# Output projection as split fp32r products, latents' low parts on GpSimd, later expert loads

## What is computed

```
z = rms_norm(x) @ w_in                      # (512, 1440): q_a, k_a, v_a, c_q, c_kv, k_rope
o_a = window_gqa(q_a, k_a, v_a, ...)        # 8 heads, 4 blocks of 128 queries, a band of keys
q   = rms_norm(c_q)  @ w_qb                 # (512, 384) @ (384, 768)
kv  = rms_norm(c_kv) @ w_kvb                # (512, 256) @ (256, 1024)
o_b = latent_attention(q, kv, k_rope)       # 8 heads, all 512 keys
o   = concat(rms_norm(o_a), rms_norm(o_b))
x   = x + o @ w_o                           # (512, 1024) @ (1024, 1024)
h2  = rms_norm(x);  x = x + expert_choice_ffn(h2, ...)   # 16 experts, 64 tokens each
mod = silu(c) @ w_mod + b_mod               # (1, 1024) @ (1024, 6144), used by the second block
```

## Time and profile before

| what | value |
|---|---|
| time, three runs | 1559.26, 1560.69, 1561.72 us; median 1560.69 |
| the profiled execution's own time | 1559.61 us |
| its span | 1557.8 us (the page's times lie inside this span) |
| busy: PE, weight load, DVE, ACT, POOL | 94%, 61%, 40%, 32%, 4% of the span |
| DMA | 310.27 MB, mean 199 GB/s |

### The profile page before, as it was taken

One profiled execution on the slowest core, in us unless ns is written; L12 is line 12 of the kernel. 1 busy time (PEld: TensorE's weight loads), 2 busy tenths in 40 slices (PEclk: granted clock), 3 DMA queues, 4 the chain that ended last, 5 costly groups with the idle time before them and its releaser, 6 DMA issues.

```text
span 1557.8 us, 17583 instructions
## 1 busy us (share of the span) xinstructions
PE 1459.2 (94%) x7133; PEld 956.3 (61%) x7133; DVE 616.2 (40%) x1188; ACT 490.8 (32%) x904; POOL 69.4 (4%) x96
## 2 busy tenths in 40 slices
PE   8988988998999999999996999988898999999998
PEld 6855466454433433333323899966686888888886
DVE  5366666334122222122115542125675443254325
ACT  6355376331001101100103412357734333123321
POOL 2000000000000000000001200000001101000100
PEclk9989999999999999999998999989999999999999
DMA  7477350427999999999995122140021332233211
GB/s 231 81 306 280 131 208 1 149 104 283 423 420 422 421 421 421 421 421 422 421 421 201 41 89 75 55 162 1 10 86 54 109 108 76 87 108 108 101 35 54
DMA packets 82738, 310.27 MB, mean 199 GB/s; under 512 B 7188, under 2 KB 43309, under 8 KB 55906
## 3 DMA queue, kind: packets, MB, share of 16 engines
q1 hardware_dynamic: 80656, 305.34, 50.2%
q10 hardware_dynamic: 1202, 2.15, 1.2%
q0 software_dynamic: 800, 1.66, 0.3%
HBM read 303.35 MB, written 5.78 MB: 198 GB/s over the span
## 4 chain that ended last, share of the span: by engine, by line
PE 73%; DMA 14%; DVE 6%; ACT 5%; issue 1%; SPq 0%; DVEq 0%; ACTq 0%
PE ps L433 13%; PE ps L434 13%; PE ps L435 13%; PE ps L805 13%; DMA sb<-in_w_gate 5%; DMA sb<-in_w_up 5%; PE ps L663 4%; DMA sb<-in_w_down 2%; PE ps L932 1%; PE ps L757 1%; DMA raw<-in_a_w_in 1%; ACT sb L1068 1%; PE ps L530 1%; PE ps L574 1%; PE ps L620 1%
## 5 line engine op out<-in xcount | busy, mean ns | idle before, releaser
L805 PE MATMUL ps<-sb 128*64 128x512 f32 x1536 | 352.5, 599 | 15.7 <-DMA sb<-in_w_gate 5.4
L805 PEld LDWEIGHTS ps<-sb 128*64 128x64 f32 x1536 | 102.9, 136 | 222.2 <-issue 178.6
L1068 ACT ACTIVATE sb<-ps 128x512 f32<-128x512 f32 (+4 forms) x176 | 90.7, 530 | 342.5 <-PE ps L757 88.3
L434 PE MATMUL ps<-r_fl,r_top 128*128 128x512 f32 x344 | 135.1, 393 | 0.0
L435 PE MATMUL ps<-r_act,r_low 128*128 128x512 f32 x344 | 134.8, 392 | 0.0
L433 PE MATMUL ps<-r_act,r_top 128*128 128x512 f32 x344 | 134.3, 390 | 0.0
L2096 DVE TENSOR_TENSOR r_low<-raw,r_top 128x2048 fp32r<-128x2048 f32 x33 | 74.2, 2289 | 78.7 <-ACT r_top L1068 78.7
L1874 DVE TENSOR_TENSOR sb<-sb,ps 128x512 f32<-128x512 f32 x64 | 43.7, 687 | 139.6 <-PE ps L794 139.6
L433 PE MATMUL ps<-r_low,r_h 128*128 128x256 f32 x288 | 82.5, 287 | 1.0 <-ACT sb L1068 1.0
L1068 ACT ACTIVATE r_top<-raw 128x2048 fp32r<-128x2048 f32 x33 | 61.4, 1907 | 69.7 <-PE ps L435 69.7
L434 PE MATMUL ps<-r_low,r_h 128*128 128x256 f32 x288 | 82.3, 286 | 0.0
(11 more groups left out here) (396 smaller groups left out, 2382.4 us busy)
## 6 DMA issues: line engine op xcount, KB each, us to landing
sb<-in_w_gate SPq DMA_DIRECT2D x64, 1024.0 KB, 25.3
sb<-in_w_up SPq DMA_DIRECT2D x64, 1024.0 KB, 26.0
sb<-in_w_down SPq DMA_DIRECT2D x64, 1024.0 KB, 26.4
sb<-in_w_mod SPq DMA_DIRECT2D x16, 1536.0 KB, 9.1
raw<-in_f_w_up SPq DMA_DIRECT2D x22, 1024.0 KB, 7.6
raw<-in_a_w_in SPq DMA_DIRECT2D x12, 1024.0 KB, 5.4
raw<-in_f_w_down SPq DMA_DIRECT2D x5, 2048.0 KB, 7.8
raw<-in_w_in SPq DMA_DIRECT2D x3, 1440.0 KB, 16.5
```

Source lines behind the costliest of these rows:

```text
L434: pe.matmul(o, a_hi, b_lo, start=False, stop=False)
L805: mm = pe.matmul(PS[64 * hf:64 * hf + 64, b * HALF:(b + 1) * HALF], lhsT(k), ring[c % RINGN][:, kk, hf * HALF:(hf + 1) * HALF], start=(k = ...
L1068: return act_(o, i_, ACT.Identity, bias=bias, scale=scale)
```

## The change

The latent and the output projection become split products, their operands being rounded (high part) and subtracted (low part) ahead. ACT rounds the latents, the latent weights and half of `w_o`; DVE rounds the other half of `w_o`; POOL makes all the low parts but two. Since `w_o` now needs the space of the rounded latents and of ring slots 0 to 4, its load waits until the last latent projection, and chunks 0 to 4 are loaded only after the last output product. The transposes of the window's queries and keys are drawn into the z product, those of the latents into window pass 0, and `mod_rows` is placed in passes 1, 2, 4, 5, 6, 7, after token tile 1 of the projections, and after `b_heads(1)`. Declarations of places and semaphores are left out below.

```diff
@@ PE: z product, in its last eighth
+                    if half == 1 and k == KD - 1:
+                        for j in range(5):
+                            b = nb(("T", j), *((("qT_" + "da"[j % 2], j),) if j < 4 else (("kz", 1), ("kz_d", 3))))
+                            for t in range(NT - 1):
+                                pe.wait_ge(*at("zqk", t))
+                                pe.transpose(bank(b)[:, t * P:(t + 1) * P], zqk[:, t, j * P:(j + 1) * P], ident)
...
-            for j in range(10):
...
+            pe.wait_ge(*at("zqk", NT - 1))
+            for j in range(5):
+                pe.transpose(bank(bank_of["T", j])[:, (NT - 1) * P:S], zqk[:, NT - 1, j * P:(j + 1) * P], ident).then_inc(*inc("pe_T", j))
+            def turn_latents(js):
+                for j in js:
+                    b = claim(5 + (j - 5) % 3, ("cT", j - 5))
+                    bank_of["T", j] = b
+                    for t in range(NT):
+                        if j == 5:
+                            pe.wait_ge(*at("zc", t))
+                        tr = pe.transpose(bank(b)[:, t * P:(t + 1) * P], zr[:, t, (j - 4) * P:(j - 3) * P], ident)
+                    tr.then_inc(*inc("pe_T", j))
@@ PE: window attention
             a_scores(0)
-            for r in range(3):
-                claim(5 + r, ("modrow", r))
+            turn_latents((5, 6, 7))
+            pe.wait_ge(*at("z_a", (3, 1)))
...
                 if b < 7:
                     a_scores(b + 1)
-                if b in (1, 2, 4, 5, 7):
-                    mod_rows((1, 2, 4, 5, 7).index(b))
+                if b == 0:
+                    turn_latents((8, 9))
+                    for r in range(3):
+                        claim(5 + r, ("modrow", r))
+                if b in (1, 2, 4, 5, 6, 7):
+                    mod_rows((1, 2, 4, 5, 6, 7).index(b))
@@ PE: latent projections (kv likewise)
-            pe.wait_ge(*at("w_qb"))
-            pe.wait_ge(*at("w_kvb"))
+            pe.wait_ge(*at("wq_l", 3))
+            pe.wait_ge(*at("cTl", 4))
...
-                        mm = pe.matmul(bank(x, 384), cqT[:, k, t * P:(t + 1) * P], w_qb[:, k, c * 384:(c + 1) * 384],
-                                       start=(k == 0), stop=(k == 2))
+                        mm = split_product(bank(x, 384), CQ_HI[k][:, c_], CQ_LO[k][:, c_], wqb_hi[:, k, c * 384:(c + 1) * 384],
+                                           wqb_lo[:, k, c * 384:(c + 1) * 384], k == 0, k == 2)
...
-            for k in range(5, KD - 1):
-                mod_rows(k)
+                if t == 1:
+                    mod_rows(6)
@@ PE: output projection
-                        mm = pe.matmul(bank(x), oT[:, k, t * P:(t + 1) * P], w_o[:, k, hf * HALF:(hf + 1) * HALF],
-                                       start=(k == 4 * part), stop=(k == 4 * part + 3))
+                        if t == 0 and hf == 0:
+                            pe.wait_ge(*at("wo_l", k))
+                            pe.wait_ge(*at(("ol_d" if k in (5, 7) else "ol_p"), k))
+                        mm = split_product(bank(x), oT_hi[k][:, c], oT_lo[k][:, c], wo_hi[:, k, hf * HALF:(hf + 1) * HALF],
+                                           wo_lo[:, k, hf * HALF:(hf + 1) * HALF], k == 4 * part, k == 4 * part + 3)
@@ ACT: t == 3 of the z statistics, before the squares of the latents
+                if t == NT - 1:
+                    turned_queries()        # qT_a of 1 and 3, two halves of kz
@@ ACT: window attention
+                if b == 0:
+                    turned_latents((0, 1, 2))   # copy(cqT[:, j, :], bank, scale=col1[...]) -> cT
                 if b < 7:
                     a_exp(b + 1)
+                if b == 0:
+                    turned_latents((3, 4))
+                for j in ((), (0, 1, 2), (3, 4))[b] if b < 3 else ():
+                    eng.wait_ge(*at("cT", j))
+                    copy(CQ_HI[j], cqT[:, j, :]).then_inc(*inc("cTh", j))
+                if 3 <= b < 7:
+                    i, c = W_HALF[b - 3]
+                    eng.wait_ge(*at(("w_qb", "w_kvb")[i]))
+                    copy(W_HI[i][:, c], W_RAW[i][:, c]).then_inc(*inc("wq_h", b - 3))
                 for i in (1, 3):
@@ ACT: latent attention
+                if u in (8, 12, 16, 20):
+                    k = u // 2 - 4
+                    if k == 0:
+                        eng.wait_ge(*at("w_o"))
+                    copy(wo_hi[:, k, :], w_o[:, k, :]).then_inc(*inc("wo_h", k))
+                if u in (9, 13, 17, 21):
+                    round_output(u // 4 - 2)    # copy(oT_hi[k][:, :], oT[:, k, :]) -> oh
             b_out(7)
+            for k in range(4, KD):
+                if k == 4:
+                    eng.wait_ge(*at("pe_Bt", 31))
+                round_output(k)
@@ DVE: t == 3 of the z statistics, and the old place
+                if t == NT - 1:
+                    for j in (0, 2): ...    # qT_d
+                    for e in range(2): ...  # the other two halves of kz
-            for j in (0, 2): ...            # qT_d
-            for j in range(5): ...          # cT
@@ DVE: latent attention, then before the first x1
+                if u in (9, 13, 17, 21):
+                    k = u // 2 - 3
+                    if k == 1:
+                        eng.wait_ge(*at("w_o"))
+                    ve.tensor_copy(wo_hi[:, k, :], w_o[:, k, :]).then_inc(*inc("wo_g", k))
...
             ve.reciprocal(rO, rO).then_inc(*inc("rO3"))
+            for k in (5, 7):
+                eng.wait_ge(*at("oh", k))
+                ve.tensor_tensor(oT_lo[k][:, :], oT[:, k, :], oT_hi[k][:, :].bitcast(F32), ALU.subtract).then_inc(*inc("ol_d", k))
@@ POOL: before it stores the context
+            for j in range(5):
+                eng.wait_ge(*at("cTh", j))
+                eng.tensor_tensor(CQ_LO[j], cqT[:, j, :], CQ_HI[j].bitcast(F32), ALU.subtract).then_inc(*inc("cTl", j))
+            for n, (i, c) in enumerate(W_HALF):     # halves of 1152, 1152, 1024, 1024 columns
+                eng.wait_ge(*at("wq_h", n))
+                eng.tensor_tensor(W_LO[i][:, c], W_RAW[i][:, c], W_HI[i][:, c].bitcast(F32), ALU.subtract).then_inc(*inc("wq_l", n))
...
+            for k in range(KD):
+                eng.wait_ge(*at(("wo_h", "wo_g")[k % 2], k))
+                eng.tensor_tensor(wo_lo[:, k, :], w_o[:, k, :], wo_hi[:, k, :].bitcast(F32), ALU.subtract).then_inc(*inc("wo_l", k))
+                if k % 2:
+                    output_rest(k // 2)     # oT_lo[k] = oT - oT_hi[k], after oh -> ol_p
+            output_rest(4)
+            output_rest(6)
@@ SP
+            sp.wait_ge(*at("pe_kv", (3, 1)))
             sp.dma_start(w_o, I["w_o"]...)
...
-            sp.wait_ge(*at("pe_mod", 15))
-            for c in range(4):
-                expert_load(c)
...
-            for c in range(4, 6):
-                expert_load(c)
+            expert_load(5)
...
-            for c in (8, 9, 12, 13):
+            for c in (0, 1, 2, 3, 4, 8, 9, 12, 13):
                 expert_load(c)
```

More of the change, by code:

```diff
@@ L242, in program @@
         w_in, w_in_lo, w_in_hi = (view(v[:, 0:KD * 1440], KD) for v in (RAW, R_LOW, R_MID))
-        w_qb = sb(W_QB, 3, 768)
-        w_kvb = sb(W_KVB, 2, 1024)
-        w_o = sb(W_O, KD, D)
+        WO_RAW, WO_HI, WO_LO = place("wo_raw", W_O, KD * D, F32), place("r_woh", 0, KD * D, F32R), place("r_wol", W_O, KD * D, F32R)
+        w_o, wo_hi, wo_lo = (view(v[:, :], KD) for v in (WO_RAW, WO_HI, WO_LO))
         w_mod = sb(0, 3, 3072)
@@ L254, in program @@
         cqT = sb(Z, 5, S)
+        CQ_HI, CQ_LO = ([place(f"r_cq{part}{j}", o + j * S, S, F32R)[:, :] for j in range(5)] for part, o in (("h", 16384), ("l", Z)))
+        W_RAW = place("qb_raw", W_QB, 2304, F32), place("kv_raw", W_KVB, 2048, F32)
+        w_qb, w_kvb = (view(W_RAW[i][:, :], 3 - i) for i in range(2))
+        W_HI = place("r_qbh", 18944, 2304, F32R), place("r_kvh", 21248, 2048, F32R)
+        W_LO = place("r_qbl", W_QB, 2304, F32R), place("r_kvl", W_KVB, 2048, F32R)
+        wqb_hi, wkv_hi = (view(W_HI[i][:, :], 3 - i) for i in range(2))
+        wqb_lo, wkv_lo = (view(W_LO[i][:, :], 3 - i) for i in range(2))
+        W_HALF = [(i, slice(h * n, (h + 1) * n)) for i, n in ((0, 1152), (1, 1024)) for h in range(2)]
         qTa = sb(QKV, 4, S)
@@ L260, in program @@
         oT = sb(T16, KD, S)
+        O_AT = [SLOT * 4 + k * S for k in range(4)] + [Z + 4608, Z + 5120, Z + 4096, SPARE]
+        oT_hi, oT_lo = ([place(f"r_o{part}{k}", o, S, F32R) for k, o in enumerate(at_)]
+                        for part, at_ in (("h", O_AT), ("l", [T16 + k * S for k in range(KD)])))
         qb = sb(QKV, NT, 768)
@@ L1126, in _, with turned_queries, turned_latents @@
             eng.wait_ge(*at("rs1"))
+            def turned_queries():
+                eng.wait_ge(*at("qcols"))
+                for j in (1, 3):
+                    eng.wait_ge(*at("pe_T", j))
+                    copy(qTa[:, j, :], bank(bank_of["T", j]), scale=qcolA).then_inc(*inc("qT_a", j))
+                eng.wait_ge(*at("pe_T", 4))
```

(22 more changed lines are left out.)

47 lines of the change are left out of this document (24 added, 23 removed).

## The result

| | median, us | lowest to highest | runs |
|---|---|---|---|
| before | 1560.95 | 1557.69 to 1564.20 | 14 |
| changed | 1567.82 | 1560.18 to 1573.02 | 14 |

The ratio is 1.0043, 95% interval 1.0032 to 1.0054: 6.7 us slower. I go on with about 5.5. The profiled execution of the changed kernel took 1570.49 us (span 1568.7, mean granted clock 0.972). It lies 2.7 above its median, that of before 1.3 under its own, so the 10.9 us between the two spans are more than the 6.7 between the medians.

A forecast was written before the change was run, and what follows sets the result against it. The experts cost what their bytes cost at 420 GB/s, so the end moves with their stream's start. Latent attention's start +6.6, its growth +8, output projection -10.5, stream +1.0: +5.1 on 1560.7 gave 1565.8 us, range 1555 to 1576.

The forecast's parts named there:

- Start of pass 0: Window attention's first transposes wait for banks 5 to 7, held until ACT's latent copies are made: +3.1 us.
- Roundings in the loop: Window passes 1 to 4: ACT's roundings between exponentials and copies all lie on the path, +4.8 us.
- `mod_rows(5)` in pass 7: Last window pass: this modulation product takes the place of the one that left, at no cost.
- Window attention with its start: Sum of all terms for the window attention, its late start included: +8.5 us, bounds +4 to +12.
- Projections: Latent projections: shorter lead of token tile 0, -1.4 us; `b_heads(0)` no longer behind modulation products and their DMA, -2.0.
- Cold start of the latent attention: After over 10 us idle, PE starts transposes and `mod_rows(7)` at the lower clock: +1.5 us (0 to 3).
- Latent attention: New roundings and POOL holding up DVE, 18 us of work and waits, under half showing: +8 us, bounds 0 to +18.
- the first rival: Latent attention: the roundings of `w_o` hide, it grows by 1 us; 1558.8 us in all, chance 0.2.
- Output projection: 64 split products faster than plain ones, less a 0.8 us wait: -10.5 us (-12 to -8).
- From W to the stream: From `w_vc`'s issue at the last output product's end (W), the expert refills start later: +1.0 us (-0.5 to +3).
- The rival with DVE held for good: Latent attention: every POOL collision and copy shows, +16 us instead of +8; 1573.8 us in all, chance 0.17.
- The one in which PE's feed is better: Window attention costs 3.5 us, not 8.5, with PE's clock up earlier and copies half hidden; 1553.8 us, chance 0.18.

The follow-up runs named there:

- roundings late: Changed kernel with ACT's nine roundings of passes 1 to 6 moved behind its copies of the turned probabilities: 1559.43 us, ratio 0.9990.
- no GpSimd: Changed kernel without GpSimd's subtractions for the output projection, high parts multiplied in place of low parts: 1560.79 us, ratio 0.9996.
- output only: Kernel before with only the changed output projection and its loads, latents as before: 1555.39 us, ratio 0.9960.
- latents only: Changed kernel with the plain output projection of before and chunks 0 to 3 loaded early again: 1571.53 us, ratio 1.0064.
- chunks late: Kernel before with only the loads of expert chunks 0 to 4 moved behind the last output product: 1560.59 us, ratio 0.9992.
- both, five products: Changed kernel with bank claim, last two latent copies and ACT's roundings placed later, five modulation products in the window attention instead of six: 1552.53 us, ratio 0.9952.

## Why the prediction was right, point by point

Forecast +5.1 us and 1565.8; measured +6.7 and +4.4. The sign, the order of size and the likeliest case were right, and its own sign of being wrong didn't show (units 8 to 22 of the latent attention took 3.0 us more). But two large terms were off in opposite directions, so that the sum came within 2 us is in part luck. In the changed kernel's profile the window attention with its start cost +16.0 and not +8.5, and the latent attention +4.7 and not +8. W came at 348.0, not at about 345, and the first latent product at 165.6, not at 158. Behind the last chunk, where the change alters nothing, the profile took 730.9 us and that of before 729.2; over all thirteen this stretch takes 727.9 to 731.7.

- **Start of pass 0: +3.1.** The cause held: the claim of banks 5 to 7 waits for the `cT`. It was +4.6 in the profile (99.27), +3.8 to +4.2 in the four others with this pass 0. The prediction ran ACT's list without a gap (which adds up to +3.0, not +3.1), with `exp(1)` from 94.3 us. In the profile it started at 95.85, since it waited for the maxima of pass 1, and these for PE's scores at 92.97.
- **Roundings in the loop: +4.8, all on the path.** The cause held, by "roundings late". From maxima to maxima the single passes were +3.1, +1.0 and +3.1 for 1 to 3 and not 1.6, 1.0 and 1.1, since in passes 1 and 3 PE's value and score matmuls ran at the lower clock: the values took 1.98 us for 1.09 and 2.83 for 1.53, the scores 2.2 and 2.6 for 1.56. I had priced gaps, not what the clock makes of them.
- **`mod_rows(5)` in pass 7 takes the place of the one that left: 0.** This step failed. With a sixth product in the window attention the last of them is asked for earlier than before, and PE waited for `w_mod`. Product and wait together cost 4.2 us of the window attention (58.8 against 54.6); the time doesn't resolve it (2.2 us by the ratios). "Pieces of `w_mod` late" stood in my bounds and not in the sum.
- **Window attention with its start: +8.5, bounds +4 to +12.** Against 149.4 for the last value matmul the four profiles are +11.4 to +17.3. The term was mis-sized by 3 to 9 us, mostly by the two points above.
- **Projections: -1.4 and -2.0.** The stretch from the last value matmul to `b_heads(0)` fell from 41.5 to 38.2 us. Right: `b_heads(0)` waits for DVE's rotation alone. One reading was off, without effect on the sum: the 6.32 us for `w_mod` are the DMA's time in the chain, and PE waited 3.8 us of it.
- **Cold start of the latent attention: +1.5.** Right in kind. To the first turned probabilities it is 10.9 us against 10.3 (11.7 in "no GpSimd"), clock 0.50 from 200 to 205 us.
- **Latent attention: +8, of which roundings and GpSimd.** The whole was +4.7 in the changed kernel, +2.5 in "output only". The part for GpSimd (a scaling is held up for the rest of a GpSimd instruction) is shown: 6.3 us on DVE. On the path 1.6 to 2.5 us of it show at the same clock, and 4.1 with the changed kernel's lower one. The 9 us of roundings on ACT and DVE (7.8 in the trace) cost nothing; here the first rival was right.
- **Output projection: -10.5.** -10.3 in every kernel that has it, and -11.1 in "no GpSimd", which spares the 0.8 us that the prediction set against the low parts.
- **From W to the stream: +1.0.** The last chunk's products start at W + 488.9 to 489.8 in nine of the ten profiles with the changed output projection ("no GpSimd" has W + 487.6), and at W + 487.2 and 487.7 in the two with early chunks. So +1 to +2, of which the late loads alone make 0.8. The rest isn't explained. A part of it may be the clock: over the 39 us behind W it was 0.87 in "no GpSimd", "latents only" and "chunks late" and 0.78 to 0.83 in the others. No run separates the two.

The rival with DVE held for good (+16 in the latent attention) fell: the scalings did grow, by 6.3 us, but the loop hid at least a third of it. The one in which PE's feed is better was nearly built in "both, five products": its window attention is what that rival wanted, by another order of the work.

## What to carry to other kernels

Work that is put on an engine in a loop through three engines costs by its place: the same nine roundings cost about 7 us between exponentials and copies (6.0 between windows at the same clock) and none that shows behind the copies, where ACT waits for PE anyway. Before a product is moved ahead, look when its operand lands, and at what a wait for it does to those behind. Where the profile shows PE at the lower clock behind gaps, price the matmuls behind a new gap at that clock as well. Set stretches side by side at the same granted clock, and take a second profile, before a difference of a few us is put down to an instruction.

## What the runs showed of the hardware

- GpSimd's subtractions hold some of VectorE's instructions until they end: a scaling of 0.49 us took up to 1.83, and a sum of 128x4, 0.156 us, took 2.08 beside a subtraction of 1024 columns. A reduction from PSUM and a reciprocal of 128x1 are untouched. Cutting GpSimd's work to 256 columns costs 18% of its own time (32.5 us against 27.5) and takes 2.8 us off VectorE.
- One order of the work gave window attentions of 62.3 to 68.1 us with each kind of PE's waits within 0.6 us, at granted clocks of 0.97 to 0.86. What I had not expected is that this spread reaches the whole: the changed kernel's executions lie 12.8 us apart, those of before 6.5.
